# Second mixer's scan: VectorE clamps the exponents of the diagonal blocks, ScalarE takes the block between the tiles without a clamp, and the squares of a group are folded to 256 columns

## The chip, the cores and the metric

The kernel runs on one core of a Trainium2 chip, as one launch. The metric is the device time of that launch in microseconds (us). The engines are called by the profile's names: PE (TensorE matmul), PEld (its weight loads, which overlap), DVE (VectorE), ACT (ScalarE), POOL (GpSimd), and SP and the DMA queues. All matrices stand in 128 partitions; "128x256" is 128 partitions by 256 elements of float32.

## What is computed

Two transformer blocks over 256 tokens of 1024 features: first a hybrid mixer and a mixture of 32 experts, then a second mixer and a convolutional MLP. The change lies in the second mixer's state space scan and in the group norm behind it:

```python
def ssd_chunked_scan(xh, dt, a, bmat, cmat):
    ...                                         # chunks of 128 tokens, 32 heads of 64, 4 groups
    a_cum = jnp.cumsum(log_a, axis=-1)
    seg = a_cum[..., :, None] - a_cum[..., None, :]
    decay_in = jnp.exp(jnp.where(causal, seg, -jnp.inf))
    cb = jnp.einsum("bclgn,bcsgn->bcgls", cc, bc)
    y_diag = jnp.einsum("bcgjls,bcsgjp->bclgjp", cb[:, :, :, None] * decay_in, x_)
    ...                                         # the state carried from chunk to chunk
def gated_group_rmsnorm(y, z, w):
    yf = (y * jax.nn.silu(z)).reshape(bsz, s, N_GROUPS, d // N_GROUPS)
    yf = yf * lax.rsqrt(jnp.mean(yf * yf, axis=-1, keepdims=True) + EPS)
    return yf.reshape(bsz, s, d) * w
```

## The kernel before

**The frame.** The second mixer is a stream of 56 "units". A unit is one tile of weights of 1 MB: SP loads it to `raw_weights`, ACT copies it to `back_w_hi` in the reduced format of the matmul (`split_hi`, L119), DVE forms the rest `back_w_lo` (`split_lo`, L123, 128x2048), and PE multiplies it with the activations in 48 matmuls (L175 to L177), or 24 for each of the two halves of the bank. ACT's `split_hi(n+3)` waits for the end of PE's unit n, since the ring has three places. A unit's result is taken from its bank by ACT (L1815) and DVE (L2049, L2054). Every engine runs its own program in the order in which it is written; they meet at semaphores only.

**The scan.** Units 28 to 43 each carry one pair of heads p = n - 28, of 16. What each engine does for pair p:

- ACT, `decays(p)`: it waits until a DMA has spread the rows of `decay_sums` (the running sums over the tokens) over the partitions, then writes for each of two heads three blocks of 128x128 into `decay`: block 0 (tokens and sources of the first tile), block 1 (tokens of the second tile, sources of the first), block 2 (both of the second). Each is `Relu(-sum + shift)` (L1850, six of them), then one `Exp` with scale -1 over all 768 columns (L1854). The Relu is a clamp: it keeps the exponent at or below zero where the causal mask will clear the value anyway. `decays(p)` stands in ACT's program one unit ahead of the pair's use. `decay` has two places; in the trace it bears the name of the tile it lies in, b_c_v.
- DVE, `weigh(p)` (L2015, 128x768): it multiplies these blocks with the masked products of B and C.
- PE, `scan_out(p)` (L2132, L2133): it waits for `weigh(p)` and multiplies the blocks with the tokens, right behind unit n.
- DVE, `y_out(p)` (L2020): it adds the skip term.

In DVE's program unit n has the order `weigh(n-28)`, `y_out(n-29)`, the gate of the unit's bank, `split_lo(n+3)`, and behind unit 37 and unit 40 four operations `group_lo` (L2028).

**The group norm.** Four pairs make a group g. POOL multiplies by z (L1776, "gate", 128x1024). ACT squares the result in two tiles of 512 columns (L1861), behind units 34, 37 and 41, and for group 3 behind the scan. POOL adds the two (L1779, 128x512) for groups 0 to 2. PE averages over the partitions with matmuls of 256 columns (`mean_squares`, L2144): two for groups 0 to 2, and four for group 3, which has no add. They stand behind units 35, 38, 42 and ahead of unit 46. ACT forms the root (`group_rstd`, L1864 to L1870), POOL applies it (L1782, "norm", 128x1024), and ACT and DVE split the result for PE's units 44 to 51.

## Time and profile before

| | |
|---|---|
| time, median of 3 runs | 1694.58 us (1693.18 to 1694.87) |
| the profiled execution | 1691.89 us, of which the span of the trace is 1690.1 us |
| PE busy | 1649.2 us (98% of the span) |
| PEld busy | 1047.2 us (62%) |
| DVE busy | 676.7 us (40%) |
| ACT busy | 580.7 us (34%) |
| POOL busy | 43.0 us (3%) |
| granted TensorE clock | 0.997 |

Busy times are sums over the execution, and matmul records overlap each other in part, so a busy PE may still be limited by its own rate. The scan is about 110 us of the span, from 1310 to 1423 us.

### The profile page before, as it was taken

Reading aid. Unit: us, or ns where it says so; the run is one execution under the profiler, and the core shown is the slowest. Engines: PE = TensorE matmul, PEld = TensorE weight load, DVE = VectorE, ACT = ScalarE, POOL = GpSimd, SP = SyncE. Lnnn points to the kernel's source line nnn. Section 1 sums busy time; section 2 is a strip of 40 time slices with the busy share of each in tenths; the row PEclk is TensorE's granted clock in tenths of the full one; section 3 lists DMA queues with packets and bytes.
Section 4 is the critical chain, followed back from the end, with each engine's and each line's share of the span. In section 5 each row is a group of like instructions: output and inputs, shape, how many; then the busy total and the mean of one; then the engine's idle time right before and its main releaser. Section 6 shows DMA issues by size and latency. Waiting matters only on the chain.

```text
span 1690.1 us, 23878 instructions
## 1 busy us (share of the span) xinstructions
PE 1649.2 (98%) x9885; PEld 1047.2 (62%) x9885; DVE 676.7 (40%) x1195; ACT 580.7 (34%) x820; POOL 43.0 (3%) x26
## 2 busy tenths in 40 slices
PE   9999999989999999999999999999999999999998
PEld 8999853333333333333333333349999989999997
DVE  4776641212121212121212121244597675666654
ACT  6655321111111111011111111144464797466433
POOL 0000000000000000000000000000100032000000
PEclk9999999999999999999999999999999999999999
DMA  8556799999999999999999999986556653555552
GB/s 269 200 199 239 293 418 426 422 410 430 431 431 432 432 431 432 431 432 431 431 430 431 430 431 430 431 311 184 180 178 222 186 172 126 177 184 184 188 188 87
DMA packets 145732, 539.45 MB, mean 319 GB/s; under 512 B 8226, under 2 KB 102878, under 8 KB 120702
## 3 DMA queue, kind: packets, MB, share of 16 engines
q1 hardware_dynamic: 143310, 534.20, 79.9%
q10 hardware_dynamic: 2352, 4.23, 0.9%
q8 instruction: 54, 0.88, 0.2%
q14 instruction: 16, 0.13, 0.0%
HBM read 537.33 MB, written 1.08 MB: 319 GB/s over the span
## 4 chain that ended last, share of the span: by engine, by line
PE 64%; DMA 12%; DVE 2%; ACT 2%; issue 1%; SPq 0%
PE bank L1501 17%; PE bank L175 10%; PE bank L177 10%; PE bank L176 9%; PE bank L1536 9%; DMA expert_weights<-in_expert_w_up_dram 6%; DMA expert_weights_late<-in_expert_w_up_dram 6%; PE bank L1476 2%; PE bank L1457 2%; PE bank L1521 2%; PE bank L1465 1%; ACT back_w_hi L119 1%; DVE back_w_lo L123 0%; PE bank L1470 0%; PE bank L2132 0%
## 5 line engine op out<-in xcount | busy, mean ns | idle before, releaser
L1394 DVE TENSOR_TENSOR pre_act<-bank,bias_now 128x512 f32<-128x512 f32 x64 | 44.0, 688 | 648.9 <-PE bank L1521 648.9
L123 DVE TENSOR_TENSOR back_w_lo<-raw_weights,back_w_hi 128x2048 fp32r<-128x2048 f32 x90 | 205.6, 2287 | 91.6 <-ACT back_w_hi L119 90.6
L1501 PE MATMUL bank<-expert_weights_late,x_gathered 128*64 128x512 f32 x1008 | 222.5, 593 | 9.4 <-DMA expert_weights_late<-in_expert_w_up_dram 9.4
L175 PE MATMUL bank<-u_hi,back_w_hi 128*128 128x256 f32 x704 | 201.2, 286 | 0.2 <-DVE u_lo L1939 0.2
L119 ACT ACTIVATE back_w_hi<-raw_weights 128x2048 fp32r<-128x2048 f32 x90 | 170.2, 1892 | 89.9 <-PE bank L177 89.6
L176 PE MATMUL bank<-u_lo,back_w_hi 128*128 128x256 f32 x704 | 199.1, 283 | 0.0
L177 PE MATMUL bank<-u_hi,back_w_lo 128*128 128x256 f32 x704 | 199.1, 283 | 0.0
L1501 PE MATMUL bank<-expert_weights,x_gathered 128*64 128x512 f32 x752 | 166.7, 593 | 7.8 <-DMA expert_weights<-in_expert_w_up_dram 7.8
L1501 PEld LDWEIGHTS bank<-expert_weights_late,x_gathered 128*64 128x64 f32 x1008 | 71.3, 137 | 157.1 <-issue 135.7
L1315 ACT ACTIVATE pre_act<-bank 128x512 f32<-128x512 f32 x32 | 19.1, 597 | 392.9 <-PE bank L1501 379.8
L175 PEld LDWEIGHTS bank<-u_hi,back_w_hi 128*128 128x128 f32 x704 | 134.9, 192 | 2.8 <-issue 2.6
L176 PEld LDWEIGHTS bank<-u_lo,back_w_hi 128*128 128x128 f32 x704 | 135.0, 192 | 0.0
L177 PEld LDWEIGHTS bank<-u_hi,back_w_lo 128*128 128x128 f32 x704 | 135.0, 192 | 0.0
L1501 PEld LDWEIGHTS bank<-expert_weights,x_gathered 128*64 128x64 f32 x752 | 53.2, 137 | 117.1 <-issue 100.1
L1536 PE MATMUL bank<-expert_weights_late,tanhs 128*64 128x512 f32 x512 | 113.4, 595 | 0.2 <-DVE tanhs L1407 0.2
L175 PE MATMUL bank<-v_hi,back_w_hi 128*128 128x256 f32 x352 | 99.9, 284 | 0.2 <-DVE v_lo L2353 0.2
L176 PE MATMUL bank<-v_lo,back_w_hi 128*128 128x256 f32 x352 | 99.6, 283 | 0.0
L177 PE MATMUL bank<-v_hi,back_w_lo 128*128 128x256 f32 x352 | 99.6, 283 | 0.0
L1333 ACT ACTIVATE bias_rows<-bank 128x512 f32<-128x512 f32 x32 | 19.1, 597 | 206.6 <-PE bank L1536 206.6
L1536 PE MATMUL bank<-expert_weights,tanhs 128*64 128x512 f32 x360 | 80.3, 594 | 0.0
L175 PE MATMUL bank<-x_hi,m_w_hi 128*128 128x256 f32 x272 | 78.1, 287 | 0.0
L176 PE MATMUL bank<-x_lo,m_w_hi 128*128 128x256 f32 x272 | 76.8, 282 | 0.0
(422 smaller groups left out, 2643.3 us busy)
## 6 DMA issues: line engine op xcount, KB each, us to landing
expert_weights_late<-in_expert_w_up_dram SPq DMA_DIRECT2D x63, 2048.0 KB, 23.8
expert_weights<-in_expert_w_up_dram SPq DMA_DIRECT2D x47, 2048.0 KB, 24.5
expert_weights_late<-in_expert_w_down_dram SPq DMA_DIRECT2D x31, 2048.0 KB, 28.0
raw_weights<-in_w_in_dram SPq DMA_DIRECT2D x55, 1024.0 KB, 5.4
expert_weights<-in_expert_w_down_dram SPq DMA_DIRECT2D x22, 2048.0 KB, 28.0
raw_weights<-in_expert_w_up_dram SPq DMA_DIRECT2D x15, 2048.0 KB, 23.0
raw_weights<-in_w_up_dram SPq DMA_DIRECT2D x22, 1024.0 KB, 5.0
raw_weights<-in_expert_w_down_dram SPq DMA_DIRECT2D x8, 2048.0 KB, 26.9
```

Source lines behind the costliest of these rows:

```text
L119: act.activation(self.w_hi[:, s, 0:size], self.s.raw[:, s, 0:size], ACT.Copy).then_inc(self.hi_done, 1)
L123: dve.tensor_tensor(self.w_lo[:, s, 0:size], self.s.raw[:, s, 0:size], self.w_hi[:, s, 0:size].bitcast(FP32), ALU.subtract).then_inc(self. ...
L175: pe.matmul(out, lhsT=ah, rhs=bh, start=start, stop=False, skip_group_check=shared)
L176: pe.matmul(out, lhsT=ah, rhs=bl, start=False, stop=False, skip_group_check=shared)
L177: return pe.matmul(out, lhsT=al, rhs=bh, start=False, stop=stop, skip_group_check=shared)
L1315: act.activation(up_rows[:, 0, :], U[0][:, :], ACT.Copy).then_inc(up_out, 1)
L1394: dve.tensor_tensor(both.rearrange("p g k n -> p (g k) n").rearrange("p a (h n) -> p a h n", h=2), TB[b][:, :].rearrange("p (a h n) -> p a ...
L1457: m = pe.matmul(TB[0][rows[c], :], lhsT=onehot[:, t, :], rhs=s.h[:, t, 512 * c:512 * c + 512], start=(t == 0), stop=(t == 1))
L1476: m = pe.matmul(s.bank[ACC + 2 * t + c][:, :], lhsT=scatter[rows[c], P * t:P * t + P], rhs=y_rows[rows[c], :], start=False, stop=True, ski ...
L1501: m = pe.matmul(up_out_rows(b, half), lhsT=xg[:, 2 * u + a, :], rhs=w[:, a, b, half, :, :], start=(first and a == 0), stop=(last and a == 1))
L1521: m = pe.transpose(TB[b][:, P * gk:P * gk + P], up_rows[:, b, gk:512:4], C("identity"))
L1536: m = pe.matmul(U[0][rows[c], :], lhsT=act_t[:, b, g, half, :], rhs=parts[half][:, g, 512 * c:512 * c + 512], start=(b + half + g == 0), s ...
```

## The change

In `decays(p)` ACT no longer clamps. The blocks 0 and 2 of both heads are now made by DVE in a new function `decay_args(p)`: four operations of 128x128 that subtract the shift and take the minimum with zero. Block 1 is taken by ACT in one operation, `Exp(sum + shift)`, for each head. Then ACT waits for the four clamped blocks (`args_ready`) and takes their `Exp` in one operation of 512 columns. The signs of the shifts follow. POOL adds the squares for all four groups, and behind that add it folds the 512 columns to 256 with a second add, so that `mean_squares` is one matmul for each group.

```diff
@@ gpsimd @@
-                if g < N_GROUPS - 1:
-                    pool.wait_ge(squared, 2 * g + 2)
-                    pool.tensor_tensor(squares[0], squares[0], squares[1], ALU.add).then_inc(squares_added, 1)
+                pool.wait_ge(squared, 2 * g + 2)
+                pool.tensor_tensor(squares[0], squares[0], squares[1], ALU.add).then_inc(pool_own, 1)
+                pool.wait_ge(pool_own, g + 1)
+                pool.tensor_tensor(squares[0][:, 0:T], squares[0][:, 0:T], squares[0][:, T:2 * T], ALU.add).then_inc(squares_added, 1)
@@ scalar, decays @@
-                    for b, c in ((0, slice(0, P)), (1, slice(P, T)), (2, slice(P, T))):
-                        own.add(act.activation(decay[:, p % 2, hh, P * b:P * b + P], row[:, c], ACT.Relu, scale=-1.0,
-                                               bias=shift[:, b, h:h + 1]))
+                    own.add(act.activation(decay[:, p % 2, hh, P:T], row[:, P:T], ACT.Exp, bias=shift[:, 1, h:h + 1]))
+                act.wait_ge(args_ready, 4 * (p + 1))
+                diagonal = decay[:, p % 2, :, :].rearrange("p h (b t) -> p h b t", b=3)[:, :, 0:3:2, :]
+                act.activation(diagonal, diagonal, ACT.Exp).then_inc(decay_ready, 1)
                 own.wait()
-                both = decay[:, p % 2, :, :].rearrange("p h b -> p (h b)")
-                act.activation(both, both, ACT.Exp, scale=-1.0).then_inc(decay_ready, 1)
@@ vector @@
+            def decay_args(p):
+
+                dve.wait_ge(shift_ready, 1)
+                dve.wait_ge(sums_loaded[p % (ROWS // 2)], 16 * (p // (ROWS // 2) + 1))
+                if p >= 2:
+                    dve.wait_ge(y_mm, p - 1)
+                for hh in range(2):
+                    h, row = 2 * p + hh, sums[:, (2 * p + hh) % ROWS, :]
+                    for b, c in ((0, slice(0, P)), (2, slice(P, T))):
+                        dve.tensor_scalar(decay[:, p % 2, hh, P * b:P * b + P], row[:, c], shift[:, b, h:h + 1], 0.0,
+                                          op0=ALU.subtract, op1=ALU.min).then_inc(args_ready, 1)
+
...
+                if n == 28:
+                    decay_args(0)
+                if 28 <= n < 43:
+                    decay_args(n - 27)
                 if n >= 28:
                     weigh(n - 28)
@@ tensor, mean_squares @@
-                if g < N_GROUPS - 1:
-                    parts = 2
-                    pe.wait_ge(squares_added, g + 1)
-                else:
-                    parts = 4
-                    pe.wait_ge(squared, 2 * g + 2)
-                for i in range(parts):
-                    m = pe.matmul(s.bank[7][:, 0:T], lhsT=C("mean512"), rhs=squares[i // 2][:, T * (i % 2):T * (i % 2) + T], start=(i == 0), stop=(i == parts - 1))
-                m.then_inc(ms_mm, 1)
+                pe.wait_ge(squares_added, g + 1)
+                pe.matmul(s.bank[7][:, 0:T], lhsT=C("mean512"), rhs=squares[0][:, 0:T], start=True, stop=True).then_inc(ms_mm, 1)
```

DVE's program around unit 38, before the change (L123 is `split_lo`, L2028 `group_lo`, L2015 `weigh`, L2020 `y_out`, L2054 the gate of the bank):

```order
L123 TENSOR_TENSOR back_w_lo<-raw_weights,back_w_hi 128x2048
L2028 SCALAR_TENSOR_TENSOR ya_lo<-x_b_c,half_norm_w,ya_hi 128x256 x4
L2015 TENSOR_TENSOR b_c_v<-b_c_v,x_b_c 128x768
L2020 SCALAR_TENSOR_TENSOR x_b_c<-x_b_c,parameter_cols,bank 128x256
L2054 SCALAR_TENSOR_TENSOR z<-z,bank 128x512
```

The same place of DVE's program after the change (L2021 is the new clamp, L2027 `weigh`, L2032 `y_out`, L2040 `group_lo`, L2070 the gate):

```order
L123 TENSOR_TENSOR back_w_lo<-raw_weights,back_w_hi 128x2048
L2040 SCALAR_TENSOR_TENSOR ya_lo<-x_b_c,half_norm_w,ya_hi 128x256 x4
L2021 TENSOR_SCALAR b_c_v<-decay_sums,decay_shift 128x128 x4
L2027 TENSOR_TENSOR b_c_v<-b_c_v,x_b_c 128x768
L2032 SCALAR_TENSOR_TENSOR x_b_c<-x_b_c,parameter_cols,bank 128x256
L2070 SCALAR_TENSOR_TENSOR z<-z,bank 128x512
```

The four clamps of the next pair stand between `split_lo` (or `group_lo`) and `weigh` in each of units 28 to 42; unit 28 has eight, for pairs 0 and 1.

POOL's program for one group, before (gate, add, norm):

```order
L1776 TENSOR_TENSOR x_b_c<-x_b_c,z 128x1024
L1779 TENSOR_TENSOR b_c_v<-b_c_v,squares 128x512
L1782 TENSOR_TENSOR x_b_c<-x_b_c,group_rstd 128x1024
```

And after:

```order
L1776 TENSOR_TENSOR x_b_c<-x_b_c,z 128x1024
L1778 TENSOR_TENSOR b_c_v<-b_c_v,squares 128x512
L1780 TENSOR_TENSOR b_c_v<-b_c_v 128x256
L1783 TENSOR_TENSOR x_b_c<-x_b_c,group_rstd 128x1024
```

The fold of 256 columns stands between the add and the norm in each of the four groups.

## Rows read from the trace of the kernel before

**Rows 1.** Windows: stretch, length, busy us of PE, PEld, DVE, ACT, POOL; clock, DMA.
```profile
1310.00:1420.00 110.00, 108.04 (x884) 100.38 (x885) 72.61 (x68) 93.27 (x166) 21.98 (x9) 1.00 0.55 166
1420.00:1460.00 40.00, 40.00 (x329) 39.36 (x328) 20.50 (x21) 19.79 (x23) 7.15 (x3) 1.00 0.48 159
```

**Rows 2.** Waits of PE, 1310 to 1460 us: total, times, longest.
```profile
PE bank L2132 <- DVE b_c_v L2015: 2.0, 3, 1.2
```

**Rows 3.** Timeline of PE: start, duration, operation, idle time before.
```profile
1349.55 0.66 PE L2132 MATMUL bank<-b_c_v 128*64 128x256 f32 x4
...
1356.59 0.66 PE L2132 MATMUL bank<-b_c_v 128*64 128x256 f32 x4 [0.23 <-DVE b_c_v L2015]
...
1363.26 1.02 PE L2144 MATMUL bank<-b_c_v,shared_constants 128*128 128x256 f32 x4
...
1364.21 0.66 PE L2132 MATMUL bank<-b_c_v 128*64 128x256 f32 x4
...
1377.70 0.66 PE L2132 MATMUL bank<-b_c_v 128*64 128x256 f32 x4
...
1386.82 0.66 PE L2132 MATMUL bank<-b_c_v 128*64 128x256 f32 x4 [1.22 <-DVE b_c_v L2015]
...
1407.65 0.66 PE L2132 MATMUL bank<-b_c_v 128*64 128x256 f32 x4 [0.52 <-DVE b_c_v L2015]
...
1415.26 0.66 PE L2132 MATMUL bank<-b_c_v 128*64 128x256 f32 x4
...
1434.43 1.02 PE L2144 MATMUL bank<-b_c_v,shared_constants 128*128 128x256 f32 x4
```

**Rows 4.** Timeline of DVE, 1347 to 1414 us.
```profile
1347.55 0.95 DVE L2015 TENSOR_TENSOR b_c_v<-b_c_v,x_b_c 128x768 f32<-128x768 f32 x1
...
1352.09 3.58 DVE L123 TENSOR_TENSOR back_w_lo<-raw_weights,back_w_hi 128x2048 fp32r<-128x2048 f32 x1 [1.12 <-ACT back_w_hi L119]
1361.04 2.06 DVE L2015 TENSOR_TENSOR b_c_v<-b_c_v,x_b_c 128x768 f32<-128x768 f32 x1
...
1368.09 0.95 DVE L2015 TENSOR_TENSOR b_c_v<-b_c_v,x_b_c 128x768 f32<-128x768 f32 x1
...
1374.47 2.29 DVE L123 TENSOR_TENSOR back_w_lo<-raw_weights,back_w_hi 128x2048 fp32r<-128x2048 f32 x1 [1.11 <-ACT back_w_hi L119]
1376.68 0.95 DVE L2015 TENSOR_TENSOR b_c_v<-b_c_v,x_b_c 128x768 f32<-128x768 f32 x1
...
1411.80 2.06 DVE L2015 TENSOR_TENSOR b_c_v<-b_c_v,x_b_c 128x768 f32<-128x768 f32 x1
```

**Rows 5.** Timeline of POOL, 1351 to 1390 us: gate, add, norm, gate, norm.
```profile
1351.11 2.41 POOL L1776 TENSOR_TENSOR x_b_c<-x_b_c,z 128x1024 f32<-128x1024 f32 x1 [73.60 <-DVE z L2054]
1359.92 2.37 POOL L1779 TENSOR_TENSOR b_c_v<-b_c_v,squares 128x512 f32<-128x512 f32 x1 [6.40 <-ACT squares L1861]
1368.17 3.14 POOL L1782 TENSOR_TENSOR x_b_c<-x_b_c,group_rstd 128x1024 f32<-128x1024 f32 x1 [5.88 <-ACT group_rstd L1870]
1371.27 2.39 POOL L1776 TENSOR_TENSOR x_b_c<-x_b_c,z 128x1024 f32<-128x1024 f32 x1
```

**Rows 6.** DVE operations with one scalar from memory: timeline, start and length of two.
```profile
583.57 0.42 DVE L1360 TENSOR_SCALAR onehot<-shared_constants,step_cols 128x64 f32<-128x64 f32 x2
...
1221.73 0.61 DVE L1963 TENSOR_SCALAR b_c_v<-b_c_v,parameter_cols 128x256 f32<-128x256 f32 x2
```

**Rows 7.** Groups of the same operations: count, busy us, mean ns of one.
```profile
L1360 DVE TENSOR_SCALAR onehot<-shared_constants,step_cols 128x64 f32<-128x64 f32 x62 | 12.9, 252 | 1.1
...
L1963 DVE TENSOR_SCALAR b_c_v<-b_c_v,parameter_cols 128x256 f32<-128x256 f32 x8 | 2.4, 349 | 0.0
```

**Rows 8.** Timeline of ACT: one `decays`, then the squares of group 3.
```profile
1375.93 1.85 ACT L1850 ACTIVATE b_c_v<-decay_sums,decay_shift 128x128 f32<-128x128 f32 x6
1377.82 0.84 ACT L1854 ACTIVATE b_c_v<-b_c_v 128x768 f32<-128x768 f32 x1
...
1430.28 0.62 ACT L1861 ACTIVATE squares<-x_b_c 128x512 f32<-128x512 f32 x1
```

More of the change, by code:

```diff
@@ L1697, in mixer2 @@
         w_dt_split, dt_heads_mm, dt_copied = sem("m3_w_dt_split"), sem("m3_dt_heads_mm"), sem("m3_dt_copied")
-        squares_added = sem("m3_squares_added")
+        squares_added, args_ready = sem("m3_squares_added"), sem("m3_args_ready")
         sums_stored = sem("m3_sums_stored")
@@ L1896, in scalar @@
                     act.wait_ge(acum_mm, 1)
-                    for b, scale in ((0, 1.0), (1, -1.0), (2, 1.0)):
-                        own.add(act.activation(shift[:, b, :], s.bank[7][:, 32 * b:32 * b + 32], ACT.Copy, scale=scale))
+                    for b in range(3):
+                        own.add(act.activation(shift[:, b, :], s.bank[7][:, 32 * b:32 * b + 32], ACT.Copy))
                     own.wait()
```

## The prediction, made before the changed kernel ran

> **What bounds the kernel now.** I read the windows first [rows 1]. From 1310 to 1420 us, the scan, PE is busy for 108.04 of 110 us at granted clock 1.00; DVE has 72.61 us of work and ACT 93.27 us. Behind the scan, to 1460 us, PE is busy for 40.00 of 40 us. So PE's own work sets the time, and what others do counts only where PE waits. Its waits in the scan are one kind: `scan_out` for `weigh`, three times, 2.0 us in all [rows 2]. That is little, and an obvious reading would be that ACT, at 85% of the stretch, is what should be relieved. PE's timeline against DVE's says otherwise, and here each pair has to be looked at.
>
> A unit with its `scan_out` takes 6.75 us (half of the 13.49 us from 1364.21 to 1377.70 [rows 3]). What matters is the margin: the start of `scan_out` less the end of its `weigh`. In an ordinary unit `weigh(5)` ends at 1347.55 + 0.95 = 1348.50 and `scan_out(5)` starts at 1349.55: 1.05 us [rows 3, 4]. For pair 7 it is 1364.21 - 1363.10 = 1.11; for pair 9, 1377.70 - 1377.63 = 0.07; for pair 14, 1415.26 - 1413.86 = 1.40. Pairs 6, 10 and 13 have none: there PE waits 0.23, 1.22 and 0.52 us [rows 3]. By distance between starts less 6.75 they lose 0.29 (1349.55 to 1356.59), 1.5 (1377.70 to 1386.82, less 0.87 for two matmuls of `mean_squares`) and about 0.6. The 0.87 is the distance from 1356.59 to 1364.21, 7.62, less 6.75.
>
> Three of these places are a collision of DVE and POOL. At 1352.09 `split_lo` takes 3.58 us in place of 2.29, and ends where it would if it started when POOL's gate (1351.11 to 1353.52) is over. At 1361.04 `weigh` takes 2.06 in place of 0.95, behind an add of POOL [rows 4, 5]. The add itself waited for DVE's `split_lo` from 1359.92 to about 1361.12, and then needs 1.17 us of its 2.37. In these rows one of the two engines stands still until the other's instruction is over.
>
> This is the rule of the Trainium skill, SBUF — State Buffer, "Who interferes with whom": the port pair that VectorE shares with GpSimd is an exclusive lock for a whole instruction, for operations with two SBUF inputs and for `tensor_scalar` in a two-port mode. The trace agrees for the first kind (2.06 against 0.95 us); the clamps would be of the second.
>
> **The change, part by part.**
>
> *ACT* loses six Relus and an Exp over 768 columns, 1375.93 to 1378.66 us: 2.73 us for a pair [rows 8]. It gets two Exps of 128 columns (0.3 each, as a sixth of 1.85) and one of 512 (0.63 by the squares of 512 columns, 0.62). So it is 1.5 us shorter a pair, but now waits for DVE's clamps, which come behind `split_lo(n+2)`. That wait is hidden: in an ordinary unit the last clamp ends some 0.8 us behind `split_lo`, ACT's Exp 0.7 later, still 0.6 ahead of the end of PE's unit, at which ACT's next work starts. If that cover were gone, ACT's `split_hi` and all behind it would slip by the excess.
>
> *DVE* gets four clamps of 128 columns ahead of each `weigh`. Two operations of 256 columns with one scalar from memory take 0.61 us, one is 349 ns, so the next starts 0.26 after the first; with 64 columns it is 0.42 - 0.252 = 0.17 [rows 6, 7]. Between the two, 0.20 for 128 columns: four put `weigh` back by **0.80 us** (bounds 0.68 and 1.04).
>
> The Trainium skill prices it lower: VectorE: DVE Perf Modes, "The TRN2 errata", gives 58 cycles plus elements over the mode's factor at 0.96 GHz, and two elements a cycle for float32 `tensor_scalar` in SBUF: an estimate of 127 ns each, 0.51 us for four. For 256 columns it gives 194 ns, where the rows show 0.26, so it lacks some 0.06 for the scalar from memory. With it the sum below would be about +1 us.
>
> *POOL* gets the fold. The gate of 1024 columns takes 2.41 us, the add of 512 by itself 1.17, so 256 take about 0.62. It comes behind the add in each group, and the lock sends it either ahead of a clamp or behind.
>
> *PE* loses one `mean_squares` matmul in each of groups 0 to 2 and three in group 3. Two cost 0.87 (above), so six save 6 x 0.435 = **2.6 us**. That is all that PE itself gains.
>
> Now the margins, with 0.80 for clamps everywhere, and for pairs 7, 10 and 14 also 0.62 + 0.05 for the fold on DVE's lock and 0.43 because PE comes earlier by a matmul:
>
> - ordinary units (ten of them): 1.05 or more - 0.80, no wait.
> - pair 6: 0.29 becomes 1.09: +0.8.
> - pair 7: 1.11 - 0.80 - 0.67 - 0.43 = -0.79: +0.75 (rounded with the next unit's phase).
> - pair 9: ACT was late here (table loads and `group_rstd`), and its relief gives DVE's `split_lo(39)` an earlier start: before it started 1374.47 - (1364.21 + 6.75) = 3.5 us behind `scan_out(8)`; with one `decays` 1.5 shorter, half of it eaten by later clamps, I take 2.8. But POOL's norm, asked for at 1368.17, got the lock only behind `weigh(8)`, at about 1368.96, and its gate followed at once [rows 4, 5]. With four clamps ahead of `weigh(8)` norm and gate come 0.8 later, and the gate then runs into `split_lo(39)`, which waits about 1.25. So 2.8 + 1.25 + 2.21 + 0.80 + 0.95 = 8.0 against 6.75: +1.3.
> - pair 10: +0.80 + 0.67 + 0.43, less about 1.0, an estimate, since two shorter `decays` (3.0 us) more than make up for ACT's lateness in unit 37: +0.9.
> - pair 13: +0.8, and an estimated 0.3 for the next gate of 2.4 us, which now ends inside the start of `split_lo(43)`: +1.1.
> - pair 14: 1.40 - 0.80 - 0.67 - 0.43 = -0.5: +0.5.
>
> Waits grow by 0.8 + 0.75 + 1.3 + 0.9 + 1.1 + 0.5 = 5.4 us. Less 2.6 that is +2.8. One cost is open at both ends: at 1368.17 the norm waited for `weigh`, but an add waiting since 1359.92 went ahead of one. With the clamps, DVE's stream between is longer, so the norms of groups 0 and 1 may get in ahead of `weigh(8)` and `weigh(11)`, which ends some 1.8 us late then, with pair 9's loss gone in exchange at the first: 2.2 more in all. No row settles which; I take half, 1.1. The sum is **+4 us**.
>
> Behind the scan: group 3's squares end at 1430.90 [rows 8], then 1.17 + 0.62 on POOL, up to 0.8 more against `group_lo`: 1433.5, and PE asks at 1434.43 [rows 3]. No wait, with 0.9 to spare. From there PE has no idle time [rows 1], so the rest moves with it.
>
> The profiled execution is 1691.89 us, 1690.1 of span and 1.8 around it, 0.16% below the median of 1694.58. By it the changed kernel takes 1695.9; on the scale of the median, **1698.6 us**.
>
> **The rivals.**
>
> *The clamps are cheap or hide (+2 to -1).* If `weigh` slips by 0.5 and not by 0.8, each of six places gives back 0.3: +4 - 1.8, and without the lock's 1.1 about +1; if it slips by nothing, 2.6 are saved less some 1.6, since a PE that comes earlier waits for the same `weigh(10)` and for the fold: -1. Time 1693.6 to 1696. For it: margins of 1.05 and more in ten of sixteen units. Against: rows 6, and the places that have no margin. The page's 127 ns belongs here.
>
> *ACT is what made DVE late (faster).* If the three waits end with ACT's work, shortening it by 1.5 a pair takes them away: 2.4 and 2.6 are saved, -5, 1689.6. It decides once the relief exceeds the 0.8 of the clamps at pairs 6, 10 and 13. Against: at pair 6 `split_lo` itself took 3.58 us, and ACT was on time; only pairs 9 and 10 had a late ACT.
>
> *The lock falls badly, or a clamp costs 0.26 (+6 to +9).* At 4 x 0.26 = 1.04 the ordinary margin of 1.05 is used up; then units without a collision wait too, and the norms of both groups go ahead of `weigh`: 1700.6 to 1703.6.
>
> *The fold comes late, not `weigh`.* If POOL gets the lock for the fold only behind the clamps and `weigh`, PE waits at `mean_squares` (some 1 us at groups 0 and 2, 0.6 at group 1) and not behind it. The sum is nearly the same, and this is part of the forecast.
>
> **How the numbers follow.** 0.2% of the time, 3.4 us, is about what a measurement of this kernel can tell from no change. Chances: forecast (+2 to +6) 0.55, of which 0.2 lie below 3.4; cheap clamps 0.22; bad lock 0.17; ACT's relief 0.06. So slower 0.35 + 0.17 = 0.52, within 0.2% 0.20 + 0.22 = 0.42, faster 0.06. The range leaves out ACT's relief and the end of the bad case: 1693.5 (-1) to 1702.5 (+8). The forecast's own is 1696.6 to 1700.6.
>
> **What would show it.** In the profile after: the clamp's start-to-start time (0.20); DVE's busy time up by 60 x 0.2 = 12 us and ACT's down by 16 x 1.5 = 24; `mean_squares` four matmuls; PE's waits in the scan from 2.0 to some 8 us, at pairs 6, 7, 9, 10, 13 and 14, released by DVE's `weigh`; ordinary units still 6.75 apart with a margin of 0.25; POOL's second gate overlapping a long `split_lo`. The prediction is wrong if `weigh` is not what PE waits for, if waits stay near 2 us, or if ACT comes late because it waits for the clamps.

## The result, and the profile after

The changed kernel takes 1698.47 us (median of 8 runs, 1695.94 to 1699.79), the kernel before on the same chip 1693.22 us (8 runs, 1691.71 to 1694.87). The ratio is 1.0024, with a 95% interval of 1.0015 to 1.0033: slower by about 4 us. (The ratio here and below is not the quotient of the two medians, which is 1.0031, or 5.3 us.) The profiled execution is 1695.94 us with a span of 1693.9, where before it was 1691.89 with 1690.1.

First the busy times of the page and, for the two stretches of [rows 1], the windows of the kernel after (the columns are those of [rows 1]).

```profile
PE 1646.9 (97%) x9873; PEld 1046.7 (62%) x9873; DVE 696.2 (41%) x1259; ACT 558.0 (33%) x756; POOL 45.5 (3%) x31
```

```profile
1310.00:1420.00 110.00, 102.23 (x828) 94.90 (x826) 86.00 (x127) 63.79 (x95) 21.61 (x11) 0.98 0.51 161
1420.00:1460.00 40.00, 39.68 (x330) 38.83 (x330) 22.01 (x22) 24.67 (x28) 10.03 (x5) 1.00 0.50 168
```

ACT has 63.8 us of work in the scan in place of 93.3, DVE 86.0 in place of 72.6, and PE, the engine that sets the time, is busy for 102.2 of the 110 us where it was for 108.0. The relief is all there, and PE stands still 5.8 us longer. The waits of PE, and then the longest wait of ACT (1300 to 1470 us; total, times, longest):

```profile
PE bank L2148 <- DVE b_c_v L2027: 8.1, 8, 1.9
...
ACT b_c_v L1853 <- DVE b_c_v L2021: 40.5, 15, 4.8
```

ACT now waits 40.5 us for DVE's clamps. In most units that costs nothing, since ACT's next work would wait for PE anyway; at units 36 and 39 it doesn't hold, as told below. PE waits for `weigh` (now L2027) eight times and 8.1 us in all, against three times and 2.0 us [rows 2]. Each place can be seen in the timeline of PE after: `scan_out` is L2148, `mean_squares` L2154.

```profile
1341.42 0.66 PE L2148 MATMUL bank<-b_c_v 128*64 128x256 f32 x4
...
1348.16 0.66 PE L2148 MATMUL bank<-b_c_v 128*64 128x256 f32 x4
...
1363.56 0.66 PE L2148 MATMUL bank<-b_c_v 128*64 128x256 f32 x4 [0.33 <-DVE b_c_v L2027]
...
1379.26 0.66 PE L2148 MATMUL bank<-b_c_v 128*64 128x256 f32 x4 [0.66 <-DVE b_c_v L2027]
...
1388.42 0.66 PE L2148 MATMUL bank<-b_c_v 128*64 128x256 f32 x4 [1.90 <-DVE b_c_v L2027]
...
1396.67 0.66 PE L2148 MATMUL bank<-b_c_v 128*64 128x256 f32 x4
...
1404.54 0.66 PE L2148 MATMUL bank<-b_c_v 128*64 128x256 f32 x4 [1.06 <-DVE b_c_v L2027]
...
1412.80 0.66 PE L2148 MATMUL bank<-b_c_v 128*64 128x256 f32 x4 [1.44 <-DVE b_c_v L2027]
...
1420.38 0.66 PE L2148 MATMUL bank<-b_c_v 128*64 128x256 f32 x4 [0.32 <-DVE b_c_v L2027]
...
1427.14 0.66 PE L2148 MATMUL bank<-b_c_v 128*64 128x256 f32 x4
...
1439.56 0.59 PE L2154 MATMUL bank<-b_c_v,shared_constants 128*128 128x256 f32 x2
```

These are pairs 4, 5, 7, 9, 10, 11, 12, 13, 14, 15 and group 3's mean. Pair 6 starts at 1355.98 (wait 1.00) and pair 8 at 1371.77 (1.38). A distance less 6.745, and less 0.435 for a `mean_squares` matmul between, is what a pair loses:

| pair | 6 | 7 | 8 | 9 | 10 | 11 | 12 | 13 | 14 | sum |
|---|---|---|---|---|---|---|---|---|---|---|
| before | 0.3 | 0 | 0 | 0 | 1.5 | 0 | 0 | 0.6 | 0 | 2.4 |
| after | 1.07 | 0.40 | 1.46 | 0.74 | 1.98 | 1.50 | 1.12 | 1.51 | 0.40 | 10.2 |

So the scan loses 7.8 us more and is given back 2.6 by six matmuls: +5.2. That is what this text calls the stage, from `scan_out(0)` to the start of unit 46: 120.3 us before (1434.43 - 1315.82 + 4 x 0.435), 125.6 after (1439.56 - 1314.43 + 0.435). The spans differ by 3.8 and not by 5.2, because `scan_out(0)` starts at 1314.43 and not at 1315.82. The change has no part in that as far as the runs show: this start lies anywhere from 1313.7 to 1320.2 in the runs below (1321.95 with the clamps doubled, behind a wait of 1.38).

The cause is visible in DVE's timeline after, in an ordinary unit and then at two collisions. Four clamps are one row (L2021).

```profile
1346.16 0.87 DVE L2021 TENSOR_SCALAR b_c_v<-decay_sums,decay_shift 128x128 f32<-128x128 f32 x4
1346.95 0.95 DVE L2027 TENSOR_TENSOR b_c_v<-b_c_v,x_b_c 128x768 f32<-128x768 f32 x1
...
1350.70 3.57 DVE L123 TENSOR_TENSOR back_w_lo<-raw_weights,back_w_hi 128x2048 fp32r<-128x2048 f32 x1 [1.11 <-ACT back_w_hi L119]
...
1367.83 3.02 DVE L2021 TENSOR_SCALAR b_c_v<-decay_sums,decay_shift 128x128 f32<-128x128 f32 x4
1370.77 0.95 DVE L2027 TENSOR_TENSOR b_c_v<-b_c_v,x_b_c 128x768 f32<-128x768 f32 x1
```

In an ordinary unit the clamps put `weigh` back by 0.79 us; it ends at 1347.90, and `scan_out(5)` starts at 1348.16: a margin of 0.26 is left of 1.05. At 1350.70 the collision with POOL's gate is the one of [rows 4, 5], and behind it there is no margin to pay the 0.79 from. At 1367.83 the clamps take 3.02 us: POOL's norm got in between two of them, as POOL's timeline shows (norm of group 0, gate of group 1, norm of group 1):

```profile
1367.90 2.47 POOL L1783 TENSOR_TENSOR x_b_c<-x_b_c,group_rstd 128x1024 f32<-128x1024 f32 x1 [5.54 <-ACT group_rstd L1870]
1372.18 2.40 POOL L1776 TENSOR_TENSOR x_b_c<-x_b_c,z 128x1024 f32<-128x1024 f32 x1 [1.81 <-DVE x_b_c L2032]
...
1392.76 2.47 POOL L1783 TENSOR_TENSOR x_b_c<-x_b_c,group_rstd 128x1024 f32<-128x1024 f32 x1 [7.12 <-ACT group_rstd L1870]
```

The norm ends at 1370.37 and `weigh(8)` at 1371.72, 2.1 us later than it would; PE waits 1.38. The same happens at 1392.69 with the norm of group 1.

### The profile page after: what moved, and what is told of

It is laid out like the page before. It is cut to its first block, busy times and chain, and to the rows that moved or that the text cites. A ratio compares the mean times of both kernels' runs of the same rounds, so it can differ in the third digit from the quotient of the medians.

```text
span 1693.9 us, 23882 instructions
## 1 busy us (share of the span) xinstructions
PE 1646.9 (97%) x9873; PEld 1046.7 (62%) x9873; DVE 696.2 (41%) x1259; ACT 558.0 (33%) x756; POOL 45.5 (3%) x31
## 4 chain that ended last, share of the span: by engine, by line
PE 61%; DMA 12%; issue 2%; ACT 2%; SPq 2%; DVE 1%; ACTq 0%
PE bank L1501 16%; PE bank L175 9%; PE bank L177 9%; PE bank L176 9%; PE bank L1536 8%; DMA expert_weights<-in_expert_w_up_dram 6%; DMA expert_weights_late<-in_expert_w_up_dram 6%; PE bank L1457 2%; PE bank L1476 2%; PE bank L1521 2%; SPq L1291 1%; ACT back_w_hi L119 1%; DVE b_c_v L2021 1%; PE bank L1465 1%; PE bank L1470 0%
## 5 line engine op out<-in xcount | busy, mean ns | idle before, releaser
L123 DVE TENSOR_TENSOR back_w_lo<-raw_weights,back_w_hi 128x2048 fp32r<-128x2048 f32 x90 | 206.2, 2293 | 87.5 <-ACT back_w_hi L119 86.4
```

Of the source, the lines that this page charges most:

```text
L123: dve.tensor_tensor(self.w_lo[:, s, 0:size], self.s.raw[:, s, 0:size], self.w_hi[:, s, 0:size].bitcast(FP32), ALU.subtract).then_inc(self. ...
```

## The experiments

Each run is named in the table as in its section; "lo late" means that four operations of DVE, `group_lo`, stand later. The theory: a DVE operation ahead of `weigh` costs its length wherever the margin at `scan_out` is used up, and the lock with POOL makes this worse at two places; ACT's relief is worth nothing. The rivals: the fold (or POOL's longer work) is what costs; the change made ACT late, since it now waits for DVE; the clamps' cost is the lock's alone. In the table "ratio" is to the kernel before on the same chip, and "waits" are PE's in the scan, for `weigh` and for the fold.

| run | median us | ratio | 95% | stage us | waits us |
|---|---|---|---|---|---|
| before | 1693.22 | 1 | | 120.3 | 2.0 + 0 |
| after | 1698.47 | 1.0024 | 1.0015 to 1.0033 | 125.6 | 8.1 + 0 |
| clamps only | 1697.44 | 1.0025 | 1.0014 to 1.0036 | 125.6 | 7.2 + 0 |
| fold only | 1692.89 | 0.9999 | 0.9991 to 1.0008 | 119.4 | 2.0 + 1.0 |
| clamps in the gap | 1694.61 | 1.0007 | 0.9998 to 1.0016 | 120.6 | 3.9 + 0.4 |
| `weigh` first | 1707.49 | 1.0076 | 1.0063 to 1.0089 | 131.7 | 7.2 + 2.6 |
| small norm | 1697.18 | 1.0025 | 1.0016 to 1.0034 | 124.5 | 7.1 + 0 |
| own wait first | 1698.21 | 1.0031 | 1.0019 to 1.0043 | 125.6 | 8.1 + 0 |
| fold, lo late | 1692.04 | 0.9992 | 0.9982 to 1.0001 | 118.6 | 0.2 + 2.2 |
| gap, lo late | 1691.19 | 0.9992 | 0.9983 to 1.0001 | 118.8 | 1.3 + 1.2 |
| group 3's fold, lo late | 1690.29 | 0.9978 | 0.9969 to 0.9987 | 117.2 | 0.2 + 0 |
| gap, group 3's fold, lo late | 1690.58 | 0.9984 | 0.9975 to 0.9993 | 118.2 | 1.3 + 0 |
| after, lo late | 1696.65 | 1.0019 | 1.0010 to 1.0028 | 123.7 | 5.9 + 0.2 |
| clamps doubled | 1709.70 | 1.0087 | 1.0071 to 1.0103 | 133.0 | 14.6 + 0 |

### The two halves apart

"Clamps only" is the changed kernel with the squares as they were before; "fold only" is the kernel before with the new squares. Against the changed kernel, the first puts this back:

```diff
-                pool.wait_ge(squared, 2 * g + 2)
-                pool.tensor_tensor(squares[0], squares[0], squares[1], ALU.add).then_inc(pool_own, 1)
-                pool.wait_ge(pool_own, g + 1)
-                pool.tensor_tensor(squares[0][:, 0:T], squares[0][:, 0:T], squares[0][:, T:2 * T], ALU.add).then_inc(squares_added, 1)
+                if g < N_GROUPS - 1:
+                    pool.wait_ge(squared, 2 * g + 2)
+                    pool.tensor_tensor(squares[0], squares[0], squares[1], ALU.add).then_inc(squares_added, 1)
...                                             # and mean_squares as it was before
```

> Only the clamps on VectorE and ScalarE's direct block; adds and mean_squares as before. If the clamps ahead of weigh are the cost: PE's waits at scan_out 8 to 9 us as in the changed kernel, and with three mean_squares pairs of matmuls and one of four back, +4 to +6 us on the kernel before. If the fold is the cost (a late second add, or its hold on DVE): waits near 3 us, +0 to +1.

> Only the fold of the squares; ScalarE's six Relus as before. If the fold costs nothing or little: 2.6 us of matmuls saved, 1 to 1.6 given back at pair 10 and at mean_squares itself, so -1 to -1.6 us on the kernel before. If the fold is what slowed the changed kernel: +3 or more.

The clamps alone are as slow as the whole change: 1.0025, stage +5.3. PE's waits are 7.2 us at pairs 6, 8, 9, 10, 11, 12 and 13 (1.00, 1.00, 0.67, 0.99, 1.39, 0.66, 1.43). The fold alone is no change in time: its stage is 0.9 shorter in place of 2.6. The waits of PE, fold only:

```profile
PE bank L2133 <- DVE b_c_v L2016: 2.0, 3, 1.2
PE bank L2139 <- POOL b_c_v L1780: 1.0, 2, 0.7
```

The three matmuls of groups 0 to 2 (1.3 us) are more than paid back: pairs 7, 10 and 14 lose 0.6, 0.7 and 0.3 more than before, in waits for the fold and for a `weigh` that PE reaches sooner. So the fold's gain is that of group 3, and the rival of the fold falls as the cause of the loss. In the stage the halves are +5.3 and -0.9, the whole is +5.2: under the clamps' waits the fold gains nothing more. One reason is the lock. In clamps only, where POOL has the add alone, the four clamps of pair 7 take 1.91 us and PE doesn't wait at pairs 7 and 14; with the fold behind the add they take 2.39, and PE waits 0.33 and 0.32.

### Where the clamps stand on DVE

"Clamps in the gap" puts each pair's clamps a unit earlier, ahead of `split_lo`, where DVE waits for ACT's `back_w_hi` (1.1 us, [rows 4]). "`weigh` first" puts them right behind `weigh`.

```diff
                 if n == 28:
                     decay_args(0)
-                if 28 <= n < 43:
-                    decay_args(n - 27)
+                    decay_args(1)
...
+                if 28 <= n < 42:
+                    decay_args(n - 26)
                 split_lo(dve, n + 3)
```

```diff
-                if 28 <= n < 43:
-                    decay_args(n - 27)
                 if n >= 28:
                     weigh(n - 28)
+                    if n < 43:
+                        decay_args(n - 27)
```

> The changed kernel with the four clamps moved in VectorE's program from ahead of weigh to between the gate of the bank and split_lo, where VectorE is idle for 1.1 to 1.3 us, one unit earlier. If the place of the clamps is the cost: weigh has its old margin of 1.05 us or more again, the norms meet only weigh, PE's waits fall to 1 to 2 us, and ScalarE's relief and the fold count: -2.5 to -4 us on the kernel before. If it is only that the two engines depend on each other, or the clamps' own work: +2 to +5 as in the changed kernel.

> The changed kernel with weigh ahead of the clamps, so that weigh is not put back, but ScalarE gets the clamps 0.9 us later and ends its Exp at or after the end of PE's unit. If the clamps cost by putting weigh back: waits of 2 to 4 us, -2 to +1 us on the kernel before. If they cost by making ScalarE wait: ScalarE's bank copies and split_hi come later still, waits over 8 us, +5 or more.

In the gap they cost 1.0007 in place of 1.0024: stage 120.6, 5.0 less than after. That is the theory's direction and not its size; I had expected the time to fall below that of before. Three things were missed. The clamps of one unit now run into POOL's gate instead of `split_lo` (DVE, clamps in the gap):

```profile
1354.04 3.10 DVE L2021 TENSOR_SCALAR b_c_v<-decay_sums,decay_shift 128x128 f32<-128x128 f32 x4
1357.06 2.28 DVE L123 TENSOR_TENSOR back_w_lo<-raw_weights,back_w_hi 128x2048 fp32r<-128x2048 f32 x1
```

Pairs 10 and 13 still wait, 1.24 and 1.37 us, where they waited 1.22 and 0.52 before the change: these waits have another source (below), and at pair 13 the clamps, started at 1405.18, met POOL's gate and took 2.45 besides. And pairs 9 and 12 wait 0.27 and 0.28: there ACT is late through a wait that the change put ahead of a table load, as the runs with `group_lo` moved will show.

`weigh` first is the slowest placing, 1.0076: of the two cases named ahead of it, the second came true, and the first, by which it would have been near no change, did not. Here the rival of a late ACT holds. ACT's `Exp` waits for clamps that stand behind `weigh`, and what follows on ACT waits with it (timeline of ACT, `weigh` first):

```profile
1379.48 0.63 ACT L1853 ACTIVATE b_c_v<-b_c_v 128x512 f32<-128x512 f32 x1 [3.31 <-DVE b_c_v L2021]
1380.13 1.28 ACT L1816 ACT_TABLE_LOAD   x1
1381.43 0.60 ACT L1816 ACTIVATE z<-bank 128x512 f32<-128x512 f32 x1
1381.92 1.91 ACT L119 ACTIVATE back_w_hi<-raw_weights 128x2048 fp32r<-128x2048 f32 x1
```

`back_w_hi` is late, so `split_lo` (1383.86), so `weigh` (1386.07), and PE waits 3.10 us at pair 9 and 3.66 at pair 12. Another 5.6 us of this run are not waits: pairs 10 and 13 start 2.85 and 2.71 late with no idle time ahead of `scan_out`, in stretches in which the granted clock was 0.50. A dependency from DVE to ACT and back closes a loop: ahead of `weigh` the clamps delay PE, behind it they delay ACT, which then delays PE more. Of the places tried, a unit earlier hurts least.

### The lock with POOL, and ACT's last wait

"Small norm" lets POOL's norm of groups 0 and 1 cover 8 of 256 columns, which leaves nearly all of these two norms out. "Own wait first" lets ACT wait for its own Exps ahead of the wait for the clamps.

```diff
+                n_cols = 8 if g < 2 else T
+                pool.tensor_tensor(xbc[:, 4 * g:4 * g + 4, 0:n_cols], xbc[:, 4 * g:4 * g + 4, 0:n_cols],
+                                   rstd[:, 0:n_cols].unsqueeze(1).to_broadcast([P, 4, n_cols]), ALU.mult).then_inc(normed, 1)
```

```diff
+                own.wait()
                 act.wait_ge(args_ready, 4 * (p + 1))
                 diagonal = decay[:, p % 2, :, :].rearrange("p h (b t) -> p h b t", b=3)[:, :, 0:3:2, :]
                 act.activation(diagonal, diagonal, ACT.Exp).then_inc(decay_ready, 1)
-                own.wait()
```

> The changed kernel, in which POOL's norm of groups 0 and 1 scales only 8 of 256 columns of each feature tile, so that it leaves most of that work out and holds POOL for well under 1 us in place of 2.4. If the norm between two clamps is what makes weigh of pairs 8 and 11 late: VectorE's clamps take 0.9 to 1.4 us there and not 3.0, PE's waits at these pairs (1.4 us, and 1.5 of slow clock in its place) vanish, and the waits in the scan fall from 8.1 to about 5 to 6: -2 to -3.5 us on the changed kernel. If the lock has no part in it: the same waits, no change of more than 0.5 us.

> The changed kernel with ScalarE's wait for its own operations moved ahead of the Exp of the clamped blocks, so that ScalarE's table load ahead of the Tanh of units 36 and 39 no longer carries the wait for PE's unit. If that wait makes ScalarE late at unit 39: the table load starts right behind the Exp, and pair 12's wait falls from 1.06 to about 0.6 us, -0.5 us on the changed kernel, within what a measurement can tell; if not, pair 12's wait stays at 1.06.

With a norm of 0.32 us the same four clamps take their ordinary time (timeline of DVE, small norm; against 1367.83 with 3.02 after):

```profile
1370.05 0.87 DVE L2022 TENSOR_SCALAR b_c_v<-decay_sums,decay_shift 128x128 f32<-128x128 f32 x4
1370.84 0.95 DVE L2028 TENSOR_TENSOR b_c_v<-b_c_v,x_b_c 128x768 f32<-128x768 f32 x1
```

The 2.15 us between 3.02 and 0.87 are the norm's, so the lock is shown, and the wait at pair 8 (1.38) is gone. But the stage gets only 1.1 shorter, where 2 to 3.5 were expected. At pair 9 the wait grows from 0.66 to 1.05. ACT's timeline says why: its `Exp` is over early now, but the table load behind it starts only when PE's unit is over, so that its 1.28 us are exposed (unit 36, small norm):

```profile
1372.68 1.28 ACT L1817 ACT_TABLE_LOAD   x1 [1.10 <-PE bank L177]
```

`split_lo(39)` starts 3.88 us behind `scan_out(8)` with it, for 3.48 after. The load at unit 39 waits in the same way, 2.57 us. And pair 11 still starts 8.23 us behind pair 10, without any wait; that is the clock, told at the end.

The place of ACT's own wait is what puts the load there. In the kernel before, it stood ahead of the `Exp`; the change moved it behind, between the `Exp` and the load. In the kernel after, the load at unit 39 starts at 1396.82, with ACT idle for 0.44 until PE's unit is over; with the own wait first it starts as soon as the `Exp` ends:

```profile
1396.82 1.28 ACT L1816 ACT_TABLE_LOAD   x1 [0.44 <-PE bank L177]
...
1396.05 1.28 ACT L1816 ACT_TABLE_LOAD   x1
```

(The first row is of the kernel after, the second of own wait first.) Pair 12's wait goes from 1.06 to 0.73, but pairs 7, 8, 9, 10 and 14 wait 0.05 to 0.07 longer each, and the stage stays at 125.6. In the changed kernel, where the load is late at one unit and by 0.44 only, moving the wait gains nothing.

### The four operations ahead of `weigh` that were there before

The waits at pairs 10 and 13 stayed in "fold only" and "clamps in the gap". What stands ahead of these `weigh`s is `group_lo`, four operations behind units 37 and 40. "Lo late" puts them behind `weigh` and `y_out` of the next unit:

```diff
                     if n > 28:
                         y_out(n - 29)
+                for g, at in ((0, 38), (1, 41)):
+                    if n == at:
+                        group_lo(g)
                 b = bank_of[n]
...
                 split_lo(dve, n + 3)
-                for g, at in ((0, 37), (1, 40)):
-                    if n == at:
-                        group_lo(g)
```

> The kernel before with the fold alone, and group_lo of groups 0 and 1 moved in VectorE's program from ahead of weigh to behind y_out, where VectorE is idle; ScalarE clamps as before. If PE's largest waits are weigh standing behind group_lo and POOL's add: waits at pairs 10 and 13 (1.2 and 0.5 us) go, the wait for the fold at group 1 too, -2.5 to -3.5 us on the kernel before. If they are ScalarE's lateness: unchanged against the fold alone, -0.5 to -1.

> Clamps in VectorE's gap ahead of split_lo, fold, and group_lo behind y_out: the two moves together. If both work by taking things out from ahead of weigh: against the clamps in the gap alone waits at pairs 10 and 13 (1.2 and 1.4 us) go, -1.5 to -3 us on the kernel before. If the clamps still cost more by the lock (they stand behind POOL's gate at pairs 6, 9 and 12) than ScalarE's relief is worth: slower than the fold with group_lo moved, by 0.5 to 2 us.

The waits for `weigh` fall to 0.2 us with the fold and to 1.3 with the clamps in the gap as well. The time doesn't follow: PE now waits 2.2 us for the fold instead (0.33, 1.21 and 0.62 at groups 0 to 2). In front of a late `weigh` the fold's wait was hidden; once `weigh` is on time, it is the fold that comes last (POOL, fold and lo late: the fold takes 1.33 where `weigh` runs, 0.80 elsewhere):

```profile
1362.28 2.36 POOL L1778 TENSOR_TENSOR b_c_v<-b_c_v,squares 128x512 f32<-128x512 f32 x1 [6.40 <-ACT squares L1862]
1364.72 1.33 POOL L1780 TENSOR_TENSOR b_c_v<-b_c_v 128x256 f32<-128x256 f32 x1
```

So the next pair folds group 3 alone, whose fold has slack, and keeps two matmuls for groups 0 to 2:

```diff
+                pool.wait_ge(squared, 2 * g + 2)
+                if g < N_GROUPS - 1:
+                    pool.tensor_tensor(squares[0], squares[0], squares[1], ALU.add).then_inc(squares_added, 1)
+                else:
+                    pool.tensor_tensor(squares[0], squares[0], squares[1], ALU.add).then_inc(pool_own, 1)
+                    pool.wait_ge(pool_own, 1)
+                    pool.tensor_tensor(squares[0][:, 0:T], squares[0][:, 0:T], squares[0][:, T:2 * T], ALU.add).then_inc(squares_added, 1)
```

> The kernel before with group_lo of groups 0 and 1 behind y_out, and the fold for group 3 alone (groups 0 to 2 with two matmuls as before). From scan_out(0) to unit 46 the kernel before takes 120.3 us. If the fold of groups 0 to 2 costs more in PE's wait at mean_squares (2.2 us in the run with the fold and group_lo moved) than the 1.3 us of matmuls it saves, and for group 3 nothing: only pair 6 still waits (0.2 us), 117.0 to 117.3 us, -3 us on the kernel before. If the wait for the fold only stands in for a wait for weigh: 118.5 or more, as with the whole fold.

> The same with the clamps on VectorE, in the gap ahead of split_lo. If ScalarE's relief is worth nothing, since PE never waits for ScalarE there, and the clamps meet POOL's gate: waits at pairs 6, 9 and 12 (0.7, 0.3, 0.3 us), 117.7 to 118.5 us, 0.5 to 1.2 slower than the run without the clamps on VectorE. If ScalarE's relief is worth something: faster than it.

Without any clamp on DVE this is the fastest version: 1690.29 us for 1693.62 of before, 0.9978 (0.9969 to 0.9987). Its PE timeline has one wait left in the scan, and the windows show PE busy for 109.55 of 110 us (108.04 before):

```profile
1310.00:1420.00 110.00, 109.55 (x898) 101.83 (x897) 73.99 (x70) 94.45 (x166) 23.08 (x9) 1.00 0.57 170
```

The 3.2 us of the stage are three matmuls (1.3) and what pairs 10 and 13 no longer lose (1.9). ACT has 94.45 us of work there, the most of all versions, and it holds nobody up. With the clamps in the gap on top, everything else equal, the stage is 1.0 longer, PE waiting 1.3 (0.74, 0.27 and 0.27 at pairs 6, 9 and 12) in place of 0.2. The two medians, 1690.29 and 1690.58, are too near to tell apart; the waits are not. So moving the clamps, at its best place of those tried, gains nothing and costs about 1 us.

Not all of this 1 us is the clamps'. Pair 6, where they meet POOL's gate, loses 0.5 more than without them. Pairs 9 and 12 lose 0.3 each (pair 10 gives back 0.2), and there DVE has ended its clamps and waits for ACT's `back_w_hi` again, for 0.32 and 0.33. ACT's own wait stands behind the `Exp` in this kernel, and the table load waits for PE again, at both units:

```profile
1371.39 1.28 ACT L1819 ACT_TABLE_LOAD   x1 [1.91 <-PE bank L177]
```

Without the clamps on DVE the same load starts at 1371.58, right behind ACT's `Exp`, though ACT has more work. So ACT's relief did make its `Exp` end early here, 1.75 us ahead of `scan_out(8)` for 0.2, and the wait behind it gave that away. The kernel with the clamps in the gap and ACT's own wait first was not run. Whether the relief would then be worth something, or the cost only sink to the 0.5 of pair 6, is open.

### The changed kernel with lo late, and with the clamps doubled

The first takes the `group_lo` edit to the changed kernel. The second writes every clamp twice, once to a spare tile, so that DVE has eight ahead of `weigh`:

```diff
+                own.wait()
...
+                        step(dve.tensor_scalar(spare[:, 2 * hh + b // 2, :], row[:, c], shift[:, b, h:h + 1], 0.0,
+                                               op0=ALU.subtract, op1=ALU.min))
                         dve.tensor_scalar(decay[:, p % 2, hh, P * b:P * b + P], row[:, c], shift[:, b, h:h + 1], 0.0,
                                           op0=ALU.subtract, op1=ALU.min).then_inc(args_ready, 1)
```

> The changed kernel with group_lo of groups 0 and 1 behind y_out, the clamps still ahead of weigh. If PE's wait of 1.90 us at pair 10 is group_lo and POOL's adds ahead of weigh: it falls to 0.4, the granted clock stays at 1.00 behind it, and pair 11 now shows as a wait of 1.4 us (the norm between two clamps) what the slow clock hid; pair 13 falls from 1.44 to 0.3. 122.5 to 123.3 us from scan_out(0) to unit 46 in place of 125.6. If the slow clock comes by itself: it is there again, with pair 11 at 8.25 us.

> The changed kernel with each clamp made twice, the first time into a spare tile that nobody reads, so that weigh comes another 0.8 us later in every unit. If a unit's margin decides: ordinary units, which have 0.26 us left in the changed kernel, now wait 0.55 each (pairs 1 or 2 to 5), and the collision places 0.8 more each: +8 to +12 us on the changed kernel. If the clamps only cost where POOL collides with them: ordinary units stay at 6.75, +3 to +5.

Lo late takes 1.9 us off the stage of the changed kernel (125.6 to 123.7), a little less than expected. Pair 10 waits 0.33 in place of 1.90, and pair 13 no longer, but now pair 11 waits 1.75: it is the lock with the norm of group 1, which the changed kernel's trace had hidden behind a slow PE. Behind that wait the clock falls once more, and pair 12 loses 1.50 without a wait.

Doubled, the clamps start 0.20 apart again (1339.79, 1339.99, ... 1341.17, `weigh` at 1341.36: eight in 1.57). PE waits ten times and 14.6 us, the stage is 7.4 longer than after, and another 1.4 is lost at pair 0 ahead of it: 8.8 in all. The ratios, 1.0087 and 1.0024, make it 10.7; the 2 us between are not explained by the scan. The ordinary units tell most:

```profile
1335.63 0.66 PE L2152 MATMUL bank<-b_c_v 128*64 128x256 f32 x4
...
1342.38 0.66 PE L2152 MATMUL bank<-b_c_v 128*64 128x256 f32 x4
...
1349.31 0.66 PE L2152 MATMUL bank<-b_c_v 128*64 128x256 f32 x4
...
1356.45 0.66 PE L2152 MATMUL bank<-b_c_v 128*64 128x256 f32 x4 [0.32 <-DVE b_c_v L2031]
```

Pairs 2 to 4 are 6.93, 6.75 and 6.93 apart from the one before, pair 5 is 7.14. The margins in the kernel after say why these differ. `weigh(4)` ends there at 1339.80 + 0.95 = 1340.75, 0.67 ahead of `scan_out(4)`; `weigh(5)` has 0.26. Four more clamps (0.78) overdraw the first by 0.11 and the second by 0.52, and the losses are 0.18 and 0.40 (pair 3 loses nothing). A single margin for all ordinary units is too coarse.

## Why the prediction was right, point by point

**The sign, the size and the mechanism.** +4 us was forecast (1698.6) and the runs gave 1698.47, or +5.3 against the 1693.22 of the same chip; the stage makes it +5.2. The path is the one named: PE waits for `weigh`, which stands behind the clamps. "Clamps only" shows it, by doing this half alone. That 1698.47 lies so near to 1698.6 is luck in part: the kernel before had a median of 1693.22 on this chip, 1.4 below the one that the forecast started from, and of the places below some were sized too large and others too small.

**The clamp.** 0.20 us from start to start was right: 0.87 for four, as 3 x 0.20 + 0.28. The Trainium skill, VectorE: DVE Perf Modes, "The TRN2 errata", gave an estimate of 127 ns; the rows show 0.20, so the measurement decides. It is about 0.07 too low here, as it was for 256 columns. That this is the price of the scalar in memory was my guess; no run has the same operation without one.

**The matmuls.** Six of them, 2.6 us, right. The sum also had PE come earlier by them at pairs 7, 10 and 14; "fold only" shows how much of it is paid back: 0.9 is left in the stage. The fold itself takes 0.80 us where 0.62 was taken, and on DVE's side of the lock 0.48 (2.39 less 1.91 at pair 7) where 0.67 was.

**The ordinary units.** A margin of 0.25 was forecast and 0.26 is there.

**The waits place by place.** Forecast for pairs 6, 7, 9, 10, 13 and 14: 0.8, 0.75, 1.3, 0.9, 1.1 and 0.5, and 1.1 for the norms at pairs 8 and 11. Measured, as growth of the loss: 0.8, 0.4, 0.7, 0.5, 0.9 and 0.4, and at pairs 8, 11 and 12 another 1.5, 1.5 and 1.1. So the six named places were oversized, 3.7 us for 5.4, and three that were named as a half chance or not at all brought 4.1 for 1.1. The errors point in opposite ways: 7.8 measured, 6.5 forecast.

- *The norm and the lock.* I left open whether the norms get in ahead of `weigh`, and took half. Both norms got in ahead of `weigh`, at 1367.90 and 1392.76. "Small norm" shows the first, and lo late bares the second with its wait of 1.75. This term of the sum is the one that was mis-sized: 1.1 was taken, and 3.0 measured at pairs 8 and 11 (2.5 in "clamps only").
- *Pair 9.* The step failed. The gate was to start behind the norm and hit `split_lo(39)`. As the norm went first, the gate started at 1372.18, waiting for `y_out(7)`, and was over at 1374.58, ahead of `split_lo` at 1375.25. ACT's relief, for which the start of `split_lo(39)` was put 2.8 behind `scan_out(8)`, brought nothing either: it is 3.48 (1375.25 - 1371.77), and was 3.5. ACT's `Exp` waited for the same clamps until 1370.88, and the table load behind it, at 1371.53, is as late against PE as before. What pair 9 lost is the 0.79 of the clamps less its margin of 0.07.
- *Pair 12.* Not foreseen, and here the prediction's own sign of being wrong came true at one place: ACT is late because it waits for the clamps. Its `Exp` at 1395.75 waited 2.48 us for clamps with the norm among them, and the second table load and `back_w_hi` come behind it. `split_lo(42)` starts 3.88 us behind `scan_out(11)`, where it was 2.54 before. I had ACT's wait for clamps down as hidden in all units. Own wait first takes 0.33 off PE's wait. In "clamps only" the load waits for nothing, but ACT's `Exp` has waited 2.47 for the clamps, `split_lo(42)` is still 3.49 behind, and PE waits 0.66.
- *Pair 11.* Of its 1.5 us nothing is a wait: the TensorE ran slow (below). In "clamps only", with no slow stretch, pair 11 waits 1.39 for the same `weigh(11)`. Either would cost nearly the same here.

**ACT's relief.** ACT's busy time fell by 22.7 us (24 forecast), DVE's rose by 19.5 (12 forecast). The difference is in how busy time is counted: a clamp that stands at the lock counts as busy, so the 64 of them have a mean of 393 ns (the group of L2021 below), and a single one is 0.28 long. The rival "ACT is what made DVE late" falls with "group 3's fold, lo late": there ACT has all its work, and the waits of pairs 10 and 13 are gone, since four operations of DVE no longer stand ahead of `weigh`. With ACT relieved on top, the stage is 118.2 for 117.2; for the open part of that see above.

```profile
L2021 DVE TENSOR_SCALAR b_c_v<-decay_sums,decay_shift 128x128 f32<-128x128 f32 x64 | 21.1, 393 | 0.0
```

**Behind the scan.** Right: group 3's add and fold end at 1438.3 (1437.48 + 0.80), PE asks at 1439.56, no wait.

**The rule of the lock.** The Trainium skill, SBUF — State Buffer, "Who interferes with whom", has it that a `tensor_scalar` in a two-port mode is held off by GpSimd's instruction. The trace agrees: 3.02 us for four clamps with a norm between them, 0.87 without. The page gives the ports to whichever instruction issues first. It doesn't say what happens when one engine already waits and the other has its next instruction ready, and that was worth more here than the rule; in the kernel before, `weigh` passed a norm that was there already (the rows at the end).

## What to carry to other kernels

Before work is moved from a busy engine to an idle one, read at each use the margin between the end of the producer and the start of its consumer on the engine that sets the time; ScalarE at 85% had held nobody up, and VectorE at 66% had, with 0.8 us more, no room left at nine pairs of sixteen. Put moved work where its engine waits for something else, not ahead of the operation that is waited for, and follow it a round further when another engine waits for it in its turn. When an operation moves, look at what its wait now stands ahead of. A gain on the bounding engine (here matmuls) is one only where nothing else is late at the next wait, which is why one fold of four paid.

## What the runs showed of the hardware that was not expected

**PE's clock falls at a long wait.** Behind the wait of 1.90 us at pair 10 the granted clock of the kernel after goes to the lower level, 1.2 GHz, and back (windows of 1 us; the clock is the third column from the end):

```profile
1389.00:1390.00 1.00, 1.00 (x9) 0.83 (x6) 0.37 (x1) 1.00 (x1) 0.00 (x0) 0.62 0.00 0
1390.00:1391.00 1.00, 1.00 (x7) 1.00 (x6) 0.52 (x1) 0.98 (x2) 0.00 (x0) 0.50 0.00 0
1391.00:1392.00 1.00, 1.00 (x7) 1.00 (x7) 1.00 (x1) 0.99 (x2) 0.00 (x0) 0.50 0.00 0
1392.00:1393.00 1.00, 1.00 (x8) 1.00 (x8) 1.00 (x3) 0.97 (x4) 0.24 (x1) 0.67 0.00 0
1393.00:1394.00 1.00, 1.00 (x11) 1.00 (x10) 1.00 (x1) 0.27 (x1) 1.00 (x1) 1.00 0.18 25
```

The unit then takes 1.5 us longer than 6.75, with no idle time. In the scans of these fourteen traces such a stretch began within 2 us of the end of eight waits (1.75, 1.90 twice, 1.97, 2.18, 2.81, 3.10 and 3.66 us) and nowhere else; at 2.18, 3.10 and 3.66 the clock fell while PE still stood. It didn't come behind two others as long (1.78 in "`weigh` first", 2.22 in "clamps doubled"), nor behind any of the waits up to 1.45. It wasn't tried by itself, so that the wait is its cause is argued, not shown, and what spares the two stays open. The traces, that of before among them, have such stretches outside the scan too. A long wait can so cost more than its length, and the slow unit hides the next late `weigh`: the loss of pair 11 can't be read from the waits.

**POOL gets in between short operations.** With four clamps back to back, a norm that comes during them runs after the one in progress. Before the change the norm of group 0 came during `weigh` and that of group 1 during `split_lo`. Each had to wait for the end of that operation, and the second was passed over besides, as POOL's and DVE's timelines of before show:

```profile
1389.27 3.82 POOL L1782 TENSOR_TENSOR x_b_c<-x_b_c,group_rstd 128x1024 f32<-128x1024 f32 x1 [4.85 <-ACT group_rstd L1870]
```

```profile
1387.67 2.28 DVE L123 TENSOR_TENSOR back_w_lo<-raw_weights,back_w_hi 128x2048 fp32r<-128x2048 f32 x1
1389.87 0.95 DVE L2015 TENSOR_TENSOR b_c_v<-b_c_v,x_b_c 128x768 f32<-128x768 f32 x1
```

It was there at 1389.27, during `split_lo`, and still `weigh` ran first. Who gets the lock between two operations can't be read from the order of asking alone. In the changed kernel, clamps only and own wait first, the norms of both groups took 2.47 us, that is, they got in after a clamp at once.

**A wait can stand on a table load.** With ACT's own wait moved behind the `Exp`, the table load for the next function starts only when PE's unit is over (1396.82, 0.44 idle ahead of it), and its 1.28 us are no longer hidden. It is the same wherever ACT is early enough in these runs: the load waits 1.10 and 2.57 us for PE in small norm, 1.92 and 2.80 with the clamps in the gap, and 1.91 and 1.85 with group 3's fold and lo late as well. "Own wait first" is the only run that takes it off, so the cause is shown at one load.
